# Second mixer: shift row by row, its first tile turned inside the dense expert stream, value sections first

## The reference

```python
def first_block(x, ...):            # mixer, PEER, final norm
    h = h + mixed @ w_out
    h = h + peer_ffn(rms_norm(h, norm2_g), w_q, sub_keys, u, v)
    return rms_norm(h, norm_f_g)

def peer_ffn(xn, ...):              # per token: 8 heads x 16 experts chosen
    act = gelu(einsum('td,thkd->thk', xb, u[expert]))
    return einsum('thk,thkd->td', g * act, v[expert])

def second_block(x, c, ...):
    shift1, scale1, gate1, shift2, scale2, gate2 = split(silu(c) @ ada_w + ada_b)
    h = rms_norm_2(x, norm1_gain) * (1.0 + scale1) + shift1
    proj = h @ w_in                 # 7 sections of 512 columns
    r_q, r_k, r_v, r_g, s_q, s_k, s_v = split(proj)
    y_ret = retention(r_q, r_k, r_v, positions)      # rotary q and k, 8 heads of 64
    y_sb = stick_breaking(rms(s_q), rms(s_k), s_v)   # 8 heads of 64, keys before the query only
    x = x + gate1 * (concat(norm(y_ret) * silu(r_g), norm(y_sb)) @ w_out)
    x = x + gate2 * peer(rms_norm_2(x, norm2_gain) * (1.0 + scale2) + shift2, ...)

def stick_breaking(q, k, v):        # z = q.k, strictly causal
    log_stay = where(mask, log_beta - z, 0.0)
    log_w = log_beta + cumsum_from_the_right(log_stay) - log_stay
    w = where(mask, exp(log_w), 0.0)
```

## Time and profile before

| | us |
|---|---|
| median of 3 runs | 3188.2 (3185.38 to 3188.89) |
| profiled execution | 3187.09 |
| its span, first to last instruction | 3185.3 |
| PE busy | 3047.1 (96%) |
| DVE busy | 2432.9 (76%) |
| end of layer 0's last expert products to start of the third projection | 1555.9 to 1593.5 |
| from there to the first retention product | 1593.5 to 1799.5 |
| retention | 1799.5 to 1837.5 |
| stick-breaking | 1837.5 to 1941.4 |

### The profile page before, as it was taken

How to read it: one execution, slowest core, us unless ns; L and a number is a source line. 1 busy time by engine, 2 the same in 40 slices (tenths; PEclk the granted TensorE clock), 3 DMA queues, 4 the chain that set the end, 5 groups by cost and what they waited for, 6 DMA issues and landing times. The chain is left out here.

```text
span 3185.3 us, 45898 instructions
## 1 busy us (share of the span) xinstructions
PE 3047.1 (96%) x16376; PEld 2036.2 (64%) x16376; DVE 2432.9 (76%) x5411; ACT 1343.7 (42%) x3424; POOL 1360.0 (43%) x1040
## 2 busy tenths in 40 slices
PE   8999999899999999999899988998899999999999
PEld 3467488766666666666344555787666666666664
DVE  6885369999899887867712275599999999878777
ACT  3333223786656555500201063226866665555100
POOL 0000000766676776766100000005576667767664
PEclk9999999999999999999899989999999999999999
DMA  9511352999999999999712101518999999999999
GB/s 307 196 53 48 135 188 90 376 343 409 408 409 394 409 409 409 409 409 409 296 53 86 50 24 40 207 63 308 330 404 408 409 403 404 409 409 409 409 409 355
DMA packets 282970, 931.22 MB, mean 292 GB/s; under 512 B 31836, under 2 KB 32492, under 8 KB 282232
## 3 DMA queue, kind: packets, MB, share of 16 engines
q0 software_dynamic: 147840, 536.96, 42.8%
q1 hardware_dynamic: 134904, 391.34, 32.3%
HBM read 921.87 MB, written 6.32 MB: 291 GB/s over the span
## 5 line engine op out<-in xcount | busy, mean ns | idle before, releaser
L811 PE MATMUL psum<-hT,mod 128*128 128x256 f32 x4096 | 957.7, 388 | 6.4 <-ACT big L1326 5.3
L811 PEld LDWEIGHTS psum<-hT,mod 128*128 128x128 f32 x4096 | 774.7, 193 | 125.1 <-issue 25.8
L1336 ACT ACTIVATE levels<-key_numbers,hT 128x128 bf16<-128x128 f32 x1792 | 567.2, 389 | 200.7 <-PE psum L864 200.3
L2056 DVE SCALAR_TENSOR_TENSOR tmp<-w,small,tmp 128x1024 f32<-128x1024 f32 x339 | 435.6, 1285 | 88.9 <-DMA w<-in_peer_up,tmp 41.5
L2036 DVE CUSTOM_DVE_ANT_0 w<-w,hn 128x1024 f32<-128x1024 f32 x342 | 409.0, 1223 | 69.8 <-DMA w<-in_peer_down,tmp 35.3
L2247 POOL DMA_INDIRECT w<-in_peer_u,tmp x172 | 237.7, 1382 | 514.0 <-DVEq L1842 402.8
L2247 POOL DMA_INDIRECT big<-in_peer_down,tmp x86 | 125.2, 1456 | 681.8 <-DVEq L1842 625.8
L821 PE MATMUL psum<-rows,big 128*128 128x512 f32 x752 | 337.1, 592 | 0.0
L864 PEld LDWEIGHTS psum<-x,levels 128*128 128x128 bf16 x6144 | 226.9, 103 | 165.3 <-issue 124.5
L1339 ACT ACTIVATE levels<-levels 128x512 bf16<-128x512 bf16 x448 | 282.3, 630 | 14.2
L864 PE MATMUL psum<-x,levels 128*128 128x32 bf16 x6144 | 235.9, 196 | 51.5 <-DVE levels L1932 21.2
(11 more groups left out here) (343 smaller groups left out, 4224.3 us busy)
## 6 DMA issues: line engine op xcount, KB each, us to landing
mod<-in_uT SPq DMA_DIRECT2D x256, 512.0 KB, 6.8
rows<-in_peer_v SPq DMA_DIRECT2D x64, 512.0 KB, 6.8
rows<-in_peer_up SPq DMA_DIRECT2D x64, 512.0 KB, 6.8
w<-in_w_in SPq DMA_DIRECT2D x14, 2048.0 KB, 8.4
srow<-in_peer_v SPq DMA_DIRECT2D x32, 512.0 KB, 6.8
tmp<-in_peer_v SPq DMA_DIRECT2D x32, 512.0 KB
srow<-in_peer_up SPq DMA_DIRECT2D x32, 512.0 KB, 6.8
tmp<-in_peer_up SPq DMA_DIRECT2D x32, 512.0 KB
```

Source lines behind the costliest of these rows:

```text
L811: last = nc.tensor.matmul(ps[4 + e % 2][:, 0:ND], ub[e % UV][:, k, :], hT[:, k, ND:SEQ], start=k == 0, stop=k == KC - 1)
L1336: last = nc.scalar.activation(hits[n % HITS][:, j * P:(j + 1) * P], keyno, ACT.Abs, bias=nibT[:, n * BATCH + j:n * BATCH + j + 1])
L2056: last = stt(y, row, c8[g % 2][:, b:b + 1], y, ALU.mult, ALU.add)
```

## The change

1. SP issues the loads of tiles 2 and 3 inside the block stream, at e = `X_BACK` = 113, in both layers; in layer 0 the shift and scale rows (1 MB) and the gain (0.5 MB) go ahead of them there. The next v load in the queue is block 118's.
2. The sections of `w_in_2` come as r_v, s_v, s_q, s_k, r_q, r_k, r_g. The first waits only for the u buffers, the second for the v buffers. The third shares the first's slot and may start at the seventh of the eight projections of r_v and s_v. The other three rows of `modulation` (1.5 MB) move behind the second decay load, since `hT0`, the turned tile 0, now lies in their place.
3. DVE makes scale and gain one row and norms tile 0 at e = `SHIFTED` = 124. Behind the loop it adds tile 2's sums first, then the last unit and tile 1, then norms tile by tile: final norm of 2, dense sums of 3, final norm of 1, normed 2, final norm of 3, normed 1, normed 3. In layer 1 the last unit comes behind the wait for tiles 2 and 3.
4. PE transposes tile 0 inside the last expert products of layer 0. Then it projects r_v and s_v tile by tile (tiles 0, 2, 1, 3), and in the four sections that are turned, the last tile is turned one projection later, behind the first tile of the next section.
5. In the stick-breaking the two masked multiplications go. PE adds to each score's diagonal part the product of the identity with `later_keys`, which is -2^100 where the key is not before the query.

The diff, cut to what is spoken of:

```diff
+SCALED, ROOTED, TURNING, SHIFTED = NKEY - 9, NKEY - 7, NKEY - 5, NKEY - 4
+X_BACK = NKEY - 15
-        OUT_FIRST = (7, 24)
+        order += [(a["w_in_2"], s * SEC) for s in (2, 6, 4, 5, 0, 1, 3)] + ...
+        OUT_FIRST = (7, 17, 24)
...
-                sp.wait_ge(u_free, (layer + 1) * len(GATHERED) * SLOTS)
-                sp.wait_ge(ga_used, (layer + 1) * QUARTERS * BATCHES)
-                for t in DENSE:
-                    sp.dma_start(x[:, t, :], x_dram[t * P:(t + 1) * P, :]).then_inc(x_back, 16)
+                    if e == X_BACK:
+                        sp.wait_ge(ga_used, (layer + 1) * QUARTERS * BATCHES)
+                        if layer == 0:
+                            sp.wait_ge(blk_done, NKEY)
+                            sp.wait_ge(top_ready, len(GATHERED))
+                            sp.dma_start(modm[:, 0:2 * D], mod_dram[0, 0:2 * D].partition_broadcast(P)).then_inc(first_in, 16)
+                            sp.dma_start(mod[:, 5, :], a["norm1_gain_2"].partition_broadcast(P)).then_inc(first_in, 16)
+                        for t in DENSE:
+                            sp.dma_start(x[:, t, :], x_dram[t * P:(t + 1) * P, :]).then_inc(x_back, 16)
...
+                        if layer == 0 and (n, c) == (1, 0):
+                            pe.wait_ge(ga_copied, QUARTERS * WIDES)
+                            transpose_tile(0)
...
+                w_rv = section()
+                pe.wait_ge(x_ready, 2)
+                project_tile(w_rv, 0)
+                w_sv = section()
+                project_tile(w_sv, 0)
+                transpose_tile(2)
+                transposes_read()
+                project_tile(w_rv, 2)
+                pe.wait_ge(x_ready, NT)
+                transpose_tile(1)
+                project_tile(w_sv, 2)
+                transposes_read()
+                project_tile(w_rv, 1)
+                transpose_tile(3)
+                project_tile(w_sv, 1)
+                transposes_read()
+                project_tile(w_rv, 3)
+                project_tile(w_sv, 3)
...
+                nc.tensor.matmul(bank[:, 0:SEQ - j * P], skT[prt, h // 2, j * P:(j + 1) * P],
+                                 sqT[prt, h // 2, j * P:SEQ], start=True, stop=False)
+                return nc.tensor.matmul(bank[:, 0:P], ident, later_keys, start=False, stop=True)
...
+            squares(3)
+            root(1, 3)
+            tile_out(sv, 0)
+            turn_tile(2)
+            tile_out(rv, 2)
...
+                    if layer == 0 and e == SHIFTED:
+                        dve.wait_ge(first_in, 32)
+                        step(stt(mod[:, 5, :], mod[:, 1, :], 1.0, mod[:, 5, :], ALU.add, ALU.mult))
+                        normed_tile(0, mod[:, 5, :], mod[:, 0, :])
...
-                    tt(wv, wv, sticks[:, 2, :], ALU.mult).then_inc(wt_ready, 1)
...
-                    tt(sv_, sv_, sticks[:, 2, :], ALU.mult).then_inc(sp_ready, 1)
```

More of the change, by code:

```diff
@@ L680, in section @@
                 return wsec[slot_of[n]]
[L682 to L688, removed]
-                    last.then_inc(pj_done, 1)
             def project_columns():
@@ L1457, in _ @@
                 turned(dst[:, :, 3 * P:4 * P])
+            for dst in (rqT, rkT):
+                for t in range(NT):
+                    turned(dst[:, :, t * P:(t + 1) * P])
+            skip(2 * NT)
             for t in range(NT):
                 bank, free = projected()
-                nc.scalar.activation(sv[:, t, :], bank, ACT.Copy).then_inc(free, 1)
+                nc.scalar.activation(rg[:, t, :], bank, ACT.Silu).then_inc(free, 1)
             for h in range(8):
@@ L1960, in peer @@
                         weigh_pair(e + WEIGHED)
-                    for n in range(units_due(e - 1), units_due(e)):
+                    for n in range(units_due(e - 1), min(units_due(e), 4 * GROUPS - 1)):
                         run_unit(layer, n)
@@ L1989, in peer @@
                         finish_half(layer, t, c, y_dense[n])
+                dve.wait_ge(x_back, 32 * (layer + 1))
+                if layer == 0:
+                    finish_dense(0, 2)
+                    run_unit(0, 4 * GROUPS - 1)
+                    deviations((2,))
+                    final_norm((2,))
+                    finish_dense(1, 3)
+                    deviations((1,))
+                    final_norm((1,))
+                    for t in (2, 3, 1):
+                        deviations((t,))
+                        if t == 3:
+                            final_norm((3,))
+                        else:
+                            normed_tile(t, mod[:, 5, :], mod[:, 0, :])
+                    deviations((3,))
+                    normed_tile(3, mod[:, 5, :], mod[:, 0, :])
+                    sines()
+                else:
+                    run_unit(1, 4 * GROUPS - 1)
+                    for n, t in enumerate(DENSE):
+                        finish_dense(n, t)
             def deviations(tiles):
@@ L2103, in rotated @@
                 tt(r, r, t3, ALU.add).then_inc(src_ready, 1)
-            deviations((1,))
-            normed_tile(1, mod[:, 5, :], mod[:, 0, :])
-            deviations(DENSE)
-            final_norm(DENSE)
-            rotated(0)
-            deviations(DENSE)
-            for t in DENSE:
-                normed_tile(t, mod[:, 5, :], mod[:, 0, :])
-            for t in range(1, NT):
-                rotated(t)
-            for t in range(NT):
-                rotated(t)
             skip(2 * NT)
             dve.wait_ge(row_in, 16 * 7)
-            dve.wait_ge(mod_in, 16)
-            step(stt(rows[:, 1, :], mod[:, 4, :], 1.0, rows[:, 1, :], ALU.add, ALU.mult))
             step(ts(srow[:, 512:576], srow[:, 512:576], 64 ** -0.5, None, ALU.mult))
+            ts(later_keys, sticks[:, 2, :], 2.0 ** 100, -2.0 ** 100, ALU.mult, ALU.add).then_inc(later_ready, 1)
             for m in range(2):
@@ L2136, in _ @@
                     tt(r3, r3, g, ALU.mult).then_inc(src_ready, 1)
+            for m in range(2):
+                for t in range(NT):
+                    rotated(t)
             skip(NT)
             for h in range(8):
+                if h == 3:
+                    dve.wait_ge(mod_in, 16)
+                    step(stt(rows[:, 1, :], mod[:, 4, :], 1.0, rows[:, 1, :], ALU.add, ALU.mult))
                 dve.wait_ge(dec_in[h % 2], 16 * (h // 2 + 1))
@@ L2185, in _ @@
                     dve.wait_ge(ar_done, m + 1)
+                    dve.wait_ge(z_used, m + 1)
                     if j == NT - 1:
```

134 lines of the change are left out of this document (55 added, 79 removed).

## The result

| | before | after |
|---|---|---|
| median, us | 3188.2 (3185.4 to 3189.9, 5 runs) | 3163.5 (3156.4 to 3169.4, 5 runs) |
| time after over time before, all runs | | 0.9922 (95%: 0.9905 to 0.9939) |
| profiled execution | 3187.1 | 3156.4 |
| block 118 of layer 0 wanted by PE | 1520.3 | 1520.9 |
| it began | 1520.3 | 1528.4 |

The changed kernel is 24.7 us faster, where 17.7 had been forecast; the time lies in the range. Its profiled execution is the fastest of the five, 7.1 us under their median, so the two profiles differ by 30.7 us and not by 24.7.

What follows compares the result with a forecast made beforehand. Before the third projection the chain on DVE and ACT was taken to bound, afterwards PE with four waits. Retention -20.4, stick-breaking +2.2 and layer 1 +0.5 give -17.7 from 3187.1: 3169.4, median 3170.5, range 3156 to 3183.

Steps and rivals of the forecast that it cites:

- The stall at block 118: Layer 0's expert stream: with half the bandwidth for q1, PE waits 8.3 us for the block behind the added transfers.
- The bound at a third of the bandwidth: Layer 0's expert stream: were q1 to get that share, a 512 KB piece takes 3.8 us and the stall is 16.
- The wait for block 127: End of layer 0's expert stream: PE's 0.89 us wait goes, since nothing is loading in front of that block.
- A: Behind layer 0's last expert product: the time when DVE has added tile 2's halves, forecast at 1561.3.
- s = 10: Behind block 118 in layer 0: everything comes 10 us later, from the 8.3 us stall plus 2 us of lower clock.
- Projections: Third projection to retention: 191.6 us instead of 206.0, four waits for turned tiles (11.6) gone; retention at 1779.1.
- Stick-breaking: Mask products on PE replace DVE's masked multiplications: net +2.2 us, range -5 to +7, stage at 106 us.
- The sum: Whole kernel: -20.4 + 2.2 + 0.5 = -17.7 us, so 3169.4 for the profiled execution and 3170.5 for the median.
- the stream hardly stalls: Rival on layer 0's expert stream: q1 gets nearly all it asks for, time 3165; chance 0.25.
- q1 gets a third: Rival on the expert stream's bandwidth: delay about 20 us, third projection at 1597.5, time about 3184; chance 0.12.
- the masks cost in full: Rival on the stick-breaking: PE's added products cost 13.4 us instead of 2.2, time 3181 to 3182; chance 0.13.
- The slower one: Rival: in the stick-breaking PE becomes the bound at the lower clock, costing 24 us more than forecast; chance 0.05.

Runs made afterwards that it cites:

- e10: Changed kernel with ACT's two copies of turned tile 2 moved ahead of s_v's tile 0 copy and the root for tile 3; 3158.5 us.
- e4: Changed kernel with its four extra transfers ahead of block 118 taken apart and spread over later blocks; 3160.0 us.
- e5: Changed kernel with layer 0's loads of tiles 2 and 3 put back behind the last v load; 3158.1 us.
- e8: Changed kernel with the last tile of the four turned sections turned right behind its projection, as before; 3181.7 us.
- e1: Kernel before with the stick-breaking's change alone (mask added by PE, no masked multiplications on DVE); 3179.0 us.
- e2: Changed kernel with the stick-breaking as it was before (masked multiplications on DVE, no mask products on PE); 3171.1 us.
- e6: Changed kernel without the 32 mask products, so with no causal mask inside the diagonal parts; 3157.9 us.
- e7: Changed kernel with each mask product on PE made twice; 3172.2 us.
- e9: Changed kernel with the 64 masked multiplications on DVE added back beside the mask products; 3170.8 us.
- e3: The changed kernel run again unchanged, for its spread; 3162.5 us.
- e12: Changed kernel with layer 0's tiles 2 and 3 loaded behind the last v load and ACT's turned tile 2 copies ahead of the root, second run; 3155.7 us.

## Why the prediction was right or wrong

**The stall at block 118: right.** 8.3 us were forecast, and 7.45 to 7.57 came in all eight profiles with this order. The half of the bandwidth held where packets were alike, 51.8%. For the shift and scale rows it didn't: q1 got 1.07 of 1.68 MB. That is the rule of the Trainium skill (DMA: Bandwidth & Descriptors, section Queues, rings and completion order), turns by packet: the trace agrees, 158 packets against 166, with 64% of the bytes. The 1.2 us that the sum had left out by it would have given 7.1. (The bound at a third of the bandwidth should have 3.9 us a piece, not 3.8.) The wait for block 127, which was to go, mostly stayed: 0.68 to 1.99 us in six of the eight. In layer 1 the wait was 2.00 (0.8 forecast; 0.7 to 2.1 in the eight profiles), which misses the "under 1 us" of the forecast's signs, and the last wait 1.48 instead of 2.13. From layer 1's queries to the end both kernels' first profiles take the same to 1.1 us.

**A and the chain of DVE and ACT: right.** A was forecast at 1561.3 and was 1560.9; the third projection at 1587.5 and was 1586.8, with ACT as the releaser. That PE waited there for ACT's order, the copy behind the root for tile 3, is shown by e10. e4 and e5 show that the transfers cost something there, but only some 3 us of s = 10 were had back (third projection 0.7 and 2.7 us earlier, retention 2.9 and 1.8): behind them stand the section loads and DVE's row of work.

**Projections: right.** 191.6 forecast, 191.7 measured; retention at 1779.1 and 1778.5. e8 shows the size of the turn's part, 16.4 us in its profile, of which the forecast named 11.6 and put the rest down to the clock. The third section's wait was 0.92, not 1.7.

**Stick-breaking: the step that failed.** The forecast had +2.2 (range -5 to +7); the profile shows -10.4, and e1 and e2 show -10.6 and -8.6 at the medians. By the forecast's own sign ("if the stick-breaking moves by more than 7 us") this part was wrong, and the stage took 92.6 us where 106 had been forecast. The failed step is "I take them as slightly more than balanced". Two things were mis-sized. A product costs 0.17 to 0.21 us between profiles with like clocks (0.15 and 0.3 at the medians of e6 and e7), not 0.42, so PE's part is 5 to 7 us, at most 10, and not 13.4. And the gaps were not half filled but went from 12.1 to 3.3 us, and the low clock of 0.90 went with them: the gaps were waits for the masked multiplications themselves, which stand twice in each step's chain, and I had priced these by what they cost DVE (0.2 us each in a row). The term's outer bound, -8.6, had been worked out and then weighted away, and the table of waits by releaser, which sets 10.0 us against the multiplications, was not used for it. e9 and e6 together show it: the multiplications alone are worth 8 to 13 us.

**The sum: right in part by luck.** e2 measures everything but the stick-breaking: 3171.1 against 3189.6, so -18.5 at the medians, where the forecast had -19.9. That part was right. The stick-breaking's term was off by 11 to 13 us and the whole by 7.0 (9.4 in e3). With -10 in place of +2.2 the sum would have been 3157 for the profiled execution (3156.4 measured) and 3158 for the median, 5 under it: the changed kernel's median lies 7.1 over its profiled execution, where the forecast had set 1.1, and that made up for a part of the error.

**The rivals.** That the stream hardly stalls, that q1 gets a third, and that the masks cost in full are refuted in the profile. The slower one, a stage at the low clock, came true as a mechanism in small: 4.7 to 6.2 us of it in some profiles, and once 75 us long in e8. It spreads the changed kernel's times and is a part of why the median lies 7 us above the profiled execution.

## What to carry to other kernels

An operation for which another engine waits is worth the wait that it causes, not what it costs its own engine. Before it is taken out, see whether the table of waits names it as releaser (L2212 and L2194 stood there with 10.0 us), and count those waits, and the low clock beside them, as gained. A transfer that is moved ahead in a full queue costs its service time, at the share that the queue gets, less the reader's slack (2.5 MB cost 7.45 us here); taking it apart moves a part of the wait to later readers (4.2 us in e4). Transpose the last tile of a group behind the next group's first product, where that costs no buffer: it was worth 16 us here.

## What the runs showed of the hardware

PE's clock can be at its low level while PE is busy almost without a gap: 75.14 of 75.70 us busy at a mean of 0.52 in e8, 10.00 of 10.00 at 0.50 in e12. Before the spell in e12 PE ran retention (products of 64 rows and of 64 columns), 33.50 of 33.50 us busy at 1.00, and then waited 0.56 us for ACT; before the one in e8 it ran projections at 1.00 and waited 0.78 us. Both waits stand in the changed kernel's first profile too, where the clock stayed at 1.00 behind them, so no row here tells why it fell. The same stretch of the same program ran at 1.00 in one profile and at 0.60 in another. So two profiles of a program can differ by 5 us at one place with no longer wait in the slower one, and a single profile doesn't tell a kernel's median to better than this.
